# Down projections of a two-kind transformer stack: each 128-row product made as two 64-row products on the row halves of TensorE's array

## What is computed

```python
# first kind, D_FF = 2816
h = rms_norm(x, ffn_norm_g[l])
x = x + (jax.nn.silu(h @ w_gate[l]) * (h @ w_up[l])) @ w_down[l]
# second kind, D_FF_2 = 4096
hf = rms_norm_2(x, g_ffn)
x = x + jnp.square(jax.nn.relu(hf @ w_up)) @ w_down
```

## Time and profile before

| | |
|---|---|
| median of three runs | 1439.38 us (1438.46 to 1440.01) |
| span of the profiled execution | 1437.9 us, 19037 instructions |
| median less the span | 1.5 us, outside of the profiled span |
| TensorE products (PE) busy | 1426.8 us, 99%, 7017 records |
| weight loads (PEld) busy | 1186.0 us, 82%, 7017 records |
| VectorE (DVE) busy | 941.6 us, 65% |
| ScalarE (ACT) busy | 746.9 us, 52% |
| mean granted TensorE clock | 0.998 |

### The profile page before, as it was taken

The page is one execution under the profiler, slowest core; times in us unless marked ns, Lnnn a source line. Parts: engine busy times, 40 slices in busy tenths (PEclk is TensorE's granted clock), DMA queues, the critical chain, the costliest instruction groups (busy, mean ns, idle before and its releaser), DMA issues.

```text
span 1437.9 us, 19037 instructions
## 1 busy us (share of the span) xinstructions
PE 1426.8 (99%) x7017; PEld 1186.0 (82%) x7017; DVE 941.6 (65%) x1167; ACT 746.9 (52%) x998; POOL 100.8 (7%) x117
## 2 busy tenths in 40 slices
PE   9999999999999999999999999999999999999997
PEld 7788888888788888888888888888888888888886
DVE  6766655446757555446799878764467998787642
ACT  7665544345855444336665445544266654455431
POOL 1211000002111000000220000000002200000001
PEclk9999999999999999999999999999999999999999
DMA  9533755455434755465355566555553555665550
GB/s 337 175 120 116 234 180 198 166 188 167 154 118 151 229 175 183 168 205 187 129 181 176 185 206 208 199 180 200 175 187 126 182 176 184 206 207 200 181 186 29
DMA packets 172582, 257.11 MB, mean 179 GB/s; under 512 B 8518, under 2 KB 90323, under 8 KB 172384
## 3 DMA queue, kind: packets, MB, share of 16 engines
q1 hardware_dynamic: 169152, 248.84, 52.0%
q10 hardware_dynamic: 3168, 6.73, 1.4%
q0 software_dynamic: 192, 0.59, 0.1%
HBM read 255.08 MB, written 1.05 MB: 178 GB/s over the span
## 4 chain that ended last, share of the span: by engine, by line
PE 95%; POOL 1%; DVE 1%; issue 1%; ACT 1%; DMA 0%; ACTq 0%; POOLq 0%; DVEq 0%
PE bank L523 24%; PE bank L525 23%; PE bank L524 23%; PE bank L1048 8%; PE bank L569 4%; PE bank L1047 4%; PE bank L552 1%; PE bank L554 1%; PE bank L553 1%; PE bank L714 1%; POOL cst L2347 1%; PE bank L905 1%; PE bank L671 1%; PE bank L697 1%; PE bank L1050 1%
## 5 line engine op out<-in xcount | busy, mean ns | idle before, releaser
L1654 DVE TENSOR_TENSOR w_lo<-w_raw,w_hi 128x2048 fp32r<-128x2048 f32 (+1 forms) x246 | 536.2, 2184 | 214.7 <-ACT w_hi L1112 211.9
L1112 ACT CAST w_hi<-w_raw 128x2048 fp32r<-128x2048 f32 (+1 forms) x246 | 446.7, 1824 | 232.0 <-PE bank L525 207.5
L523 PE MATMUL bank<-w_hi,hT 128*128 128x512 f32 (+1 forms) x1056 | 418.4, 396 | 0.0
L525 PE MATMUL bank<-w_hi,hT 128*128 128x512 f32 (+1 forms) x1056 | 411.3, 389 | 0.0
L524 PE MATMUL bank<-w_lo,hT 128*128 128x512 f32 (+1 forms) x1056 | 410.7, 389 | 0.0
L525 PEld LDWEIGHTS bank<-w_hi,hT 128*128 128x128 f32 x1056 | 198.6, 188 | 41.4
L523 PEld LDWEIGHTS bank<-w_hi,hT 128*128 128x128 f32 x1056 | 198.8, 188 | 40.2 <-issue 2.3
L524 PEld LDWEIGHTS bank<-w_lo,hT 128*128 128x128 f32 x1056 | 199.0, 188 | 38.1
L1048 PE MATMUL bank<-hT,w_hi 128*128 128x512 f32 x512 | 178.3, 396 | 0.2
L1047 PE MATMUL bank<-hT,w_lo 128*128 128x256 f32 x448 | 125.1, 279 | 0.0
L2288 POOL TENSOR_TENSOR stat<-stat,cst 128x2 f32<-128x2 f32 (+4 forms) x24 | 44.8, 1869 | 960.1 <-DVE stat L1703 831.5
(11 more groups left out here) (271 smaller groups left out, 1603.0 us busy)
## 6 DMA issues: line engine op xcount, KB each, us to landing
w_raw<-in_w_gate SPq DMA_DIRECT2D x108, 512.0 KB, 3.9
w_raw<-in_w_up SPq DMA_DIRECT2D x108, 512.0 KB, 4.5
w_raw<-in_w_down SPq DMA_DIRECT2D x104, 512.0 KB, 4.4
w_raw<-in_w_in SPq DMA_DIRECT2D x86, 512.0 KB, 4.6
w_raw<-in_w_out SPq DMA_DIRECT2D x16, 512.0 KB, 4.2
w_raw<-in_w_branch SPq DMA_DIRECT2D x32, 256.0 KB, 2.8
w_raw<-in_w_o SPq DMA_DIRECT2D x16, 512.0 KB, 4.3
bgate<-in_b_gate ACTq DMA_DIRECT2D x16, 256.0 KB, 3.3
```

Source lines behind the costliest of these rows:

```text
L523: pe.matmul(o, hi[:, kt, rows_of(r)], w_hi[:, s, j, 0:cols], start=begin, stop=False)
L525: mm = pe.matmul(o, lo[:, kt, rows_of(r)], w_hi[:, s, j, 0:cols], start=False, stop=end)
L1112: act.copy(w_hi[:, s, 0:kts, :], w_raw[:, s, 0:kts, :]).then_inc(hi_ready, 1)
L1654: dve.tensor_tensor(w_lo[:, s, 0:kts, :], w_raw[:, s, 0:kts, :], w_hi[:, s, 0:kts, :].bitcast(F32), ALU.subtract).then_inc(lo_ready, 1)
```

## The change

`by_row_halves` makes one product as two: partitions 0 to 63 of both operands into the block's bank `a[r]`, partitions 64 to 127 into the score bank `score[r]`, which is free at this point of the program. `halved_product` is `slab_product` with it, and `rows_in_turn` uses it too. Of each layer's down projection it takes all slabs of block 0, and slabs 2 and on of block 1; slabs (1, 0) and (1, 1) remain as they were, and ahead of (1, 2) TensorE waits until block 0 has been read out. VectorE now adds four banks for a block instead of two: first the score bank, then, after a wait on a new semaphore `half_added`, the block's bank. Nothing else moves.

```diff
+            def by_row_halves(banks, stationary, moving, begin, end):
+
+                for c in range(2):
+                    at = slice(c * HD, (c + 1) * HD)
+                    mm = pe.matmul(banks[c][:, :], stationary[at, :], moving[at, :], start=begin[c], stop=end)
+                return mm
+
+            def halved_product(a, hi, lo, kts, first, opens, last, between=None):
+
+                pe.wait_ge(lo_ready, q.next("slab") + RING)
+                s = (q.index("slab") - 1) % RING
+                for j, kt in enumerate(kts):
+                    for r in range(R):
+                        banks, end = (a[r], score[r]), last and j == len(kts) - 1
+                        begin = (first and j == 0, opens and j == 0)
+                        by_row_halves(banks, hi[:, kt, rows_of(r)], w_hi[:, s, j, :], begin, False)
+                        by_row_halves(banks, hi[:, kt, rows_of(r)], w_lo[:, s, j, :], (False, False), False)
+                        mm = by_row_halves(banks, lo[:, kt, rows_of(r)], w_hi[:, s, j, :], (False, False), end)
+                mm.then_inc(slab_used, 1)
...
@@ the first kind, on TensorE @@
-                        slab_product(a, hid1T_hi, hid1T_lo, kts, NB, n == 0, n == 5)
+                        if b == 0 or n > 1:
+                            if (b, n) == (1, 2):
+                                read_out(q.now("blk") - 1)
+                            halved_product(a, hid1T_hi, hid1T_lo, kts, n == 0, n == 2 * b, n == 5)
+                        else:
+                            slab_product(a, hid1T_hi, hid1T_lo, kts, NB, n == 0, False)
...
@@ the second kind, on TensorE @@
                         if (b, n) == (1, 7):
-                            rows_in_turn(a, hid2T_hi, hid2T_lo, range(28, 32))
+                            rows_in_turn(a, hid2T_hi, hid2T_lo, kts)
+                        elif b == 0 or n > 1:
+                            if (b, n) == (1, 2):
+                                read_out(q.now("blk") - 1)
+                            halved_product(a, hid2T_hi, hid2T_lo, kts, n == 0, n == 2 * b, n == 7)
                         else:
-                            slab_product(a, hid2T_hi, hid2T_lo, range(4 * n, 4 * n + 4), NB, n == 0, n == 7)
+                            slab_product(a, hid2T_hi, hid2T_lo, kts, NB, n == 0, False)
...
@@ on VectorE @@
+            def add_halves(b):
+
+                a = block_of()
+                for r in range(R):
+                    dve.tensor_tensor(x[:, r, b * NB:(b + 1) * NB], x[:, r, b * NB:(b + 1) * NB],
+                                      score[r][:, :], ALU.add).then_inc(half_added, 1)
+                for r in range(R):
+                    dve.wait_ge(half_added, q.next("half"))
+                    ins = dve.tensor_tensor(x[:, r, b * NB:(b + 1) * NB], x[:, r, b * NB:(b + 1) * NB],
+                                            a[r][:, :], ALU.add)
+                ins.then_inc(acc_free, 1)
...
                 def add_row(a, b, r):
-                    return dve.scalar_tensor_tensor(x[:, r, b * NB:(b + 1) * NB], a[r][:, :],
-                                                    stat[:, S_X2 + r:S_X2 + r + 1],
-                                                    x[:, r, b * NB:(b + 1) * NB], ALU.mult, ALU.add)
+                    add_scaled(score, b, r).then_inc(half_added, 1)
+                    dve.wait_ge(half_added, q.next("half"))
+                    return add_scaled(a, b, r)
```

More of the change, by code:

```diff
@@ L365, in build @@
         hid_lo = sem("hid_lo")
+        half_added = sem("half_added")
         row_out = sem("row_out")
@@ L535, in rows_in_turn @@
                     for j, kt in enumerate(kts):
[L536 to L539, removed]
+                        banks, end = (a[r], score[r]), j == len(kts) - 1
+                        by_row_halves(banks, hi[:, kt, rows_of(r)], w_hi[:, s, j, :], (False, False), False)
+                        by_row_halves(banks, hi[:, kt, rows_of(r)], w_lo[:, s, j, :], (False, False), False)
+                        mm = by_row_halves(banks, lo[:, kt, rows_of(r)], w_hi[:, s, j, :], (False, False), end)
                     mm.then_inc((row_out, slab_used)[r], 1)
@@ L1079, in _ @@
                             pe.wait_ge(hid_lo, q.next("hid", 2))
+                        kts = range(4 * n, 4 * n + 4)
                         if (b, n) == (1, 7):
-                            rows_in_turn(a, hid2T_hi, hid2T_lo, range(28, 32))
+                            rows_in_turn(a, hid2T_hi, hid2T_lo, kts)
[3 more added lines that the diff above has]
+                            halved_product(a, hid2T_hi, hid2T_lo, kts, n == 0, n == 2 * b, n == 7)
                         else:
-                            slab_product(a, hid2T_hi, hid2T_lo, range(4 * n, 4 * n + 4), NB, n == 0, n == 7)
+                            slab_product(a, hid2T_hi, hid2T_lo, kts, NB, n == 0, False)
                         if b == 1 and n == 1 and l < DEPTH - 1:
@@ L1792, in _ @@
                                           turn_hi=4 + 4 + 11 + 4, squares=9, rstd=7, act_done=11, scores=16,
-                                          decay=RH, probs=DH, gated=2, step=STEPS_DVE1)):
+                                          decay=RH, probs=DH, gated=2, half=4, step=STEPS_DVE1)):
                 ahead = iter(KTS1[AHEAD:] + KTS1[:AHEAD])
@@ L1961, in _ @@
                 used(6)
-                add_x(0)
+                add_halves(0)
                 splits(1)
@@ L1967, in _ @@
                 used(6)
-                add_x(1)
+                add_halves(1)
             for l in q.layers(dict(slab=len(KTS2), used=len(KTS2), row=1, blk=BLOCKS2, turn=TURNS2,
-                                          turn_hi=2 + 1 + 4 + 4 + 4, squares=5, rstd=4, act_done=10, hid=UPS, scores=12,
+                                          turn_hi=2 + 1 + 4 + 4 + 4, half=4, squares=5, rstd=4, act_done=10, hid=UPS, scores=12,
                                           probs=12, branch_hi=3, layer_in=64, bgate0=64, bgate1=64, step=STEPS_DVE2),
@@ L2227, in hidden_lo, with add_scaled, add_row @@
                                       hid2T_hi[:, bass.ds(at, 2), :].bitcast(F32), ALU.subtract).then_inc(hid_lo, 1)
-                def add_row(a, b, r):
-                    return dve.scalar_tensor_tensor(x[:, r, b * NB:(b + 1) * NB], a[r][:, :],
+                def add_scaled(src, b, r):
+                    return dve.scalar_tensor_tensor(x[:, r, b * NB:(b + 1) * NB], src[r][:, :],
                                                     stat[:, S_X2 + r:S_X2 + r + 1],
                                                     x[:, r, b * NB:(b + 1) * NB], ALU.mult, ALU.add)
+                def add_row(a, b, r):
+                    add_scaled(score, b, r).then_inc(half_added, 1)
+                    dve.wait_ge(half_added, q.next("half"))
+                    return add_scaled(a, b, r)
                 splits(1)
```

## The result

The changed kernel takes 1445.26 us (median of 4 runs, 1444.54 to 1445.64) against 1438.99 us of the kernel before in the same comparison (4 runs, 1438.46 to 1440.01). The ratio is 1.0039, 95% interval 1.0027 to 1.0051: slower by 0.4%, where 1434.5 us and a gain were forecast. The median lies 0.26 us outside the stated range. The kernel before ran beside the experiments too; over all its 48 runs its median is 1439.92 us, so the loss is better taken as 5.3 us than as 6.3. The profiled run took 1445.48 us with a span of 1443.7, so 1.8 us lie outside the span, and the same to within 0.1 us in the other runs listed; the 1.5 us of the table before compare a median with the span of one execution, and nothing in the forecast hangs on them.

A forecast was written before the change was run, and what follows sets the result against it. TensorE, busy for 99% of the span, was taken as the bound. Faster products -9.5, changes of mode +3.8 and a bare add +0.8 made -4.9 us, from 1439.4 to 1434.5 us; range 1431.5 to 1445.0.

The forecast's parts named there:

- the pace of a pair: Down projections: two fp32r halves run together and take 0.218 us, against 0.2266 us for one full-height product.
- the term of -9.5 us: Down projections: gain over 1104 products, each going from 0.2266 to 0.218 us.
- rival A: Down projections: a pair of halves keeps 0.2266 us, leaving only costs of +4.6 us, 1444.0 us; chance 0.33.
- the upper bound: Down projections: a pair takes at most 0.2266 us, if the 0.013 us beside the columns belong to type fp32r.
- So halves do run together: TensorE: float32 rows of the trace before show both halves overlapping, a pair taking 0.216 to 0.22 us.
- Changes of mode: TensorE, between full height and halves: 10 entries at 0.206 us, exits at 0.15 or 0.20 us, together +3.8 us.
- VectorE: 16 more adds of 0.68 or 0.75 us, 14 beside products; the bare last one costs +0.8 us.
- The margin at the layer's end: End of the first kind's second layer: after two more adds and the wait, 1.0 us remain before TensorE needs x.
- B: Down projections: a pair takes 0.220 to 0.225 us, -2.7 to +2.8 us, about 1439 us; chance 0.11.
- C: Down projections: a pair is slower than the full product by 0.007 to 0.013 us, 1452 to 1458 us; chance 0.05.
- D: Down projections: fp32r halves don't overlap, or a half's load can't overlap its product; +110 us, about 1550; chance 0.02.
- 22% more PE records: Expected sign in the changed kernel's trace: PE records grow by 22% as 1104 products become 2208.

The follow-up runs named there:

- run 5c: Kernel before with 1248 full-height down-projection products in bf16 instead of fp32r, stationary operand packed or spread: 1438.59 us packed, 1438.85 us spread.
- run 6: Slab (0, 2) of the first kind's down projection read as float32: 1468.51 us at full height in the kernel before, 1475.99 us by halves in the changed kernel.
- run 3: Changed kernel with the same half products in another order, three of one half, then three of the other: 1445.06 us, ratio 1.0035.
- run 2: Changed kernel with only even-numbered slabs halved (and the second kind's last): 624 halved products instead of 1104, 47 mode changes instead of 19; 1451.74 us.
- run 1: Changed kernel with its products at full height again, the same banks, adds and waits kept: 1440.62 us, ratio 1.0003 to the kernel before.
- 4: Changed kernel with only the first half of each halved product made, partitions 64 to 127 left out, VectorE's adds kept: 1444.52 us, ratio 1.003.

## Why the prediction was wrong

**The step that failed** is the pace of a pair: "I take 0.218, between the two readings for pairs, since line 867 is the nearest row in all but the type". The runs put 0.2267 in its place, the term of -9.5 us is 0, and the outcome is rival A, which had a chance of 0.33 and 1444.0 us. The reading of the rows for float32, 0.216, was right; carrying it over to fp32r was not. Its own evidence was in the text: full-height float32 passes take 0.215, the same as pairs of halves. A row that shows the same pace with and without the thing that is to be priced prices it at nothing. I compared an fp32r product at full height with a float32 pass at half height, so two things differed, and I booked the whole difference to the height.

**The reason given for the upper bound** ("if the 0.013 us belong to the type") was off as well. bf16 has nearly all of them (run 5c). They come with each product and its load where a column takes one cycle; float32, with two cycles a column, shows 2.4 ns (run 6). The outcome is that of the upper bound, the explanation isn't.

**"So halves do run together"**: right. The pairs in the trace and run 3 show it.

**Changes of mode**, +3.8 us: right in kind, a little small. Counted 19 at 0.15 to 0.206; measured 4.2 us by the trace, 0.22 each (the ways in, put at 0.206, take 0.23 to 0.25), and 0.23 each for the 28 additional ones of run 2.

**VectorE**, 14 adds covered and the last bare, +0.8 us: right. 0.78 in the chain, and 0.8 by the spans of run 1. The margin at the layer's end, put at 1.0 us, is 1.5.

**The sum of A** came out as 4.2 + 0.8 = 5.0 us against 4.6. From the 1439.4 us that the prediction started from, this gives 1444.4, inside the stated range of up to 1445.0. The measured median is 0.9 us above that: 0.5 is the start itself (1439.9 over all runs of the kernel before), the rest is within the scatter of four runs. So it was chance that the time fell just outside the range and not just inside; the mechanism of the forecast was wrong either way. Rivals B, C and D did not occur; a pair does not cost more than the full product.

**A sign that was miscounted.** "22% more PE records" doesn't follow from the prediction's own count: 1104 more on 7017 are 16%, and 16% it was.

## What to carry to other kernels

Splitting a full-height product into row halves didn't shorten it: the halves run side by side, but each at the pace of the whole (0.2267 us), and every switch between halved and full products costs about 0.2 us. Row halves gain where two products of 64 rows are there to begin with, since the two then share the time of one. What would shorten a stream of products here is fewer of them, with as many moving columns as fit (run 5b: the same columns in twice as many products, +16.3 us). When an unseen form is priced from its nearest rows, look for the pair of rows that differs in the one property alone, before taking a row that differs in two.

## What the runs showed of the hardware that was not expected

- A product with its own weight load takes 13.3 ns beside its columns at a granted clock of 1.00: 0.2267 us for 512 columns at 128 rows and at 64, 0.1200 for 256, 0.225 to 0.226 for 512 in bf16. The duration of the load (188 ns in fp32r, 96 in bf16) hardly matters. A float32 pass of 512 columns takes 0.4291 us, 2.4 ns over 1024 cycles, at either height.
- A change between full and half height costs 0.15 to 0.25 us at each place, with one half in use or with both (the changed kernel, runs 2 and 4).
- A product with 96 stationary columns is slower than one with 128: 0.230 against 0.2266 us, 4.2 us on the kernel with 1296 of them. Its cause is open.
- The two row halves aren't held to one order: with three products of one half issued ahead of three of the other, the records still pair up (run 3).
